# The near bias of the prompt's attention A added by VectorE instead of by identity matmuls

## The reference: what is computed

```python
logits = jnp.einsum('btkgd,btjkd->btkgj', qg, k_sel).astype(f32) * (D_A ** -0.5)
rel = s_pos[idx] - t_pos[None, :, None]
bias = bias_a[t5_bucket(rel)].astype(f32)
...
logits = jnp.where(valid[:, :, None, None, :], logits + bias, NEG)
p = jax.nn.softmax(logits, axis=-1).astype(v.dtype)
o = jnp.einsum('btkgj,btjkd->btkgd', p, v_sel)
```

## Time and profile before

| | |
|---|---|
| time before, median of 3 runs | 3327.85 us (3327.27 to 3331.41) |
| profiled execution: its time, its span | 3328.81 us, 3327.0 us |
| busy over the span | PE 94%, PEld 83%, DVE 41%, ACT 27%, POOL 25% |
| attention A of the prompt, units 0 to 63 | about 2203 to 2402 us of the span |
| last landmark before it | PE's matmuls of the projection end at 2188 us |

### The profile page before, as it was taken

One profiled execution on the slowest core, in us unless ns is written; L12 is line 12 of the kernel. 1 busy time (PEld: TensorE's weight loads), 2 busy tenths in 40 slices (PEclk: granted clock), 3 DMA queues, 4 the chain that ended last, 5 costly groups with the idle time before them and its releaser, 6 DMA issues. The chain is left out here.

```text
span 3327.0 us, 46645 instructions
## 1 busy us (share of the span) xinstructions
PE 3114.0 (94%) x17789; PEld 2770.6 (83%) x17789; DVE 1356.6 (41%) x2253; ACT 913.3 (27%) x1905; POOL 838.4 (25%) x613
## 2 busy tenths in 40 slices
PE   5969999999999999999999999979867999989997
PEld 5969998898989889998999999867656999878875
DVE  5002565484848169501444444047643121120322
ACT  4112212223131131112333343135433111131422
POOL 1222221221212212222222222124312222133453
PEclk7989999999999999999999999979978999999999
DMA  4453222322222313333333333132126333263453
GB/s 148 84 106 88 78 77 59 81 61 74 65 71 65 84 51 105 87 90 98 97 110 104 100 108 88 57 105 77 54 68 195 121 107 121 69 232 90 158 161 104
DMA packets 380821, 324.23 MB, mean 97 GB/s; under 512 B 39016, under 2 KB 339592, under 8 KB 377144
## 3 DMA queue, kind: packets, MB, share of 16 engines
q1 hardware_dynamic: 362888, 267.40, 28.7%
q10 hardware_dynamic: 17776, 54.65, 5.0%
HBM read 243.16 MB, written 78.88 MB: 97 GB/s over the span
## 5 line engine op out<-in xcount | busy, mean ns | idle before, releaser
L627 PE MATMUL banks<-h_hi,w_in_tile_hi 128*128 128x288 f32 (+4 forms) x2608 | 590.8, 332 | 32.2 <-POOL w_in_tile_lo L510 29.8
L510 POOL TENSOR_TENSOR w_in_tile_lo<-w_in_tile_raw,w_in_tile_hi 128x512 fp32r<-128x512 f32 x228 | 298.0, 1309 | 1174.2 <-ACT w_in_tile_hi L530 1174.2
L627 PE MATMUL banks<-h_lo,w_in_tile_hi 128*128 128x288 f32 (+4 forms) x2608 | 588.0, 331 | 0.0
L627 PE MATMUL banks<-h_hi,w_in_tile_lo 128*128 128x288 f32 (+4 forms) x2608 | 587.2, 331 | 0.0
L627 PEld LDWEIGHTS banks<-h_hi,w_in_tile_hi 128*128 128x128 f32 (+1 forms) x2608 | 442.3, 188 | 67.8 <-issue 34.1
L627 PEld LDWEIGHTS banks<-h_lo,w_in_tile_hi 128*128 128x128 f32 (+1 forms) x2608 | 446.9, 188 | 35.6 <-issue 0.4
L627 PEld LDWEIGHTS banks<-h_hi,w_in_tile_lo 128*128 128x128 f32 (+1 forms) x2608 | 446.7, 188 | 35.7 <-issue 0.4
L530 ACT CAST w_in_tile_hi<-w_in_tile_raw 128x512 fp32r<-128x512 f32 x228 | 141.6, 621 | 1008.6 <-PE banks L627 937.0
L792 DVE MAX8 top<-score 128x8 f32<-128x384 f32 (+6 forms) x224 | 247.1, 1103 | 33.0 <-DVE score L795 1.1
L1220 PE MATMUL banks<-h_hi,w_in_tile_hi 128*128 128x288 f32 (+1 forms) x1056 | 234.4, 330 | 9.7 <-PEq L133 5.5
L795 DVE MATCH_REPLACE8 score<-top,score 128x384 f32<-128x384 f32 (+6 forms) x224 | 243.0, 1085 | 0.0
(11 more groups left out here) (245 smaller groups left out, 4368.9 us busy)
## 6 DMA issues: line engine op xcount, KB each, us to landing
w_in_tile_raw<-in_w_in SPq DMA_DIRECT2D x312, 256.0 KB, 2.9
w_out_tile_raw<-in_w_out SPq DMA_DIRECT2D x128, 256.0 KB, 2.9
product<-spill ACTq DMA_DIRECT2D x48, 544.0 KB, 3.4
work<-product SPq DMA_DIRECT2D x32, 544.0 KB, 6.5
product<-g_spill ACTq DMA_DIRECT2D x22, 544.0 KB, 2.7
g_q_raw<-product SPq DMA_DIRECT2D x68, 128.0 KB, 2.8
merged<-work ACTq DMA_DIRECT2D x16, 544.0 KB, 7.7
x_rows<-in_x_prompt SPq DMA_DIRECT2D x8, 1024.0 KB, 5.2
```

The source lines that it names most:

```text
L510: pool.tensor_tensor(s.w_lo[:, q, :, :], s.w_raw[:, q, :, :], s.w_hi[:, q, :, :].bitcast(F32), ALU.subtract).then_inc(lo_made, 1)
L627: last = pe.matmul(ps[0:m, 3 * slot + c, 0:w], w_[:, q, kq, 0:m], h_[:, k, t0:t0 + w], start=(k == 0 and w_ is s.w_hi and h_ is s.h_hi), s ...
```

## The change

For the prompt alone, the two identity matmuls on the near table go, and with them the split of the table (two casts on ACT, two subtractions on DVE, the tiles near_hi and near_lo) and the waits of PE for it. DVE takes the logits with a new function `take_prompt`: the far columns of a chunk as before, the near columns with a scalar_tensor_tensor (logits + far + near), which keeps no maximum; the maximum over the near columns comes from a tensor_reduce over `prob`, and a second one, behind a new wait (`near_max`), joins it to the maxima of the far parts. The sample keeps its path.

```diff
             else:
                 k_lo_of(0)
                 q_lo_of(0)
-                for part, heads in enumerate(table_parts):
-                    near_lo_of(part, heads)
...
+            def take_prompt(n):
+                u = units[n][1]
+                if n in (0, PER):
+                    dve.wait_ge(table_in[n // PER], 16)
+                w_all = width[units[n][0]]
+                near_at = max(0, w_all - NEAR)
+                far_chunks = 0
+                for j, (c0, w) in enumerate(chunks(n)):
+                    c = first_chunk[n] + j
+                    n0 = min(max(c0, near_at), c0 + w)
+                    dve.wait_ge(logits_done, c + 1)
+                    if n0 > c0:
+                        far_chunks += 1
+                        last = dve.tensor_scalar(prob[:, n % RING, c0:n0], ps[:, c % 3, 0:n0 - c0], far[:, u:u + 1],
+                                                 None, ALU.add, ALU.max, accum_out=chunk_max[:, n % RING, j:j + 1])
+                    if n0 < c0 + w:
+                        t0 = n0 - (w_all - NEAR)
+                        last = dve.scalar_tensor_tensor(out=prob[:, n % RING, n0:c0 + w], in0=ps[:, c % 3, n0 - c0:w],
+                                                        scalar=far[:, u:u + 1], in1=near[:, u, t0:t0 + c0 + w - n0],
+                                                        op0=ALU.add, op1=ALU.add)
+                    last.then_inc(chunk_out, 1)
+                dve.wait_ge(chunk_out, first_chunk[n + 1])
+                dve.tensor_reduce(chunk_max[:, n % RING, far_chunks:far_chunks + 1], prob[:, n % RING, near_at:w_all], AX.X,
+                                  ALU.max).then_inc(near_max, 1)
+                dve.wait_ge(near_max, n + 1)
+                dve.tensor_reduce(neg_max[:, n % RING:n % RING + 1], chunk_max[:, n % RING, 0:far_chunks + 1], AX.X, ALU.max,
+                                  negate=True).then_inc(max_made, 1)
...
                     n0, n1 = max(c0, w_all - NEAR_W), c0 + w
-                    if n0 < n1:
+                    if sample and n0 < n1:
                         t0 = n0 - (w_all - NEAR_W)
                         for part in (near_hi, near_lo):
                             pe.matmul(bank[:, n0 - c0:w], s.ident_r[:, :], part[:, u, t0:t0 + n1 - n0], start=False,
```

More of the change, by code:

```diff
@@ L1350, in attend_a @@
         near = sb("near", [P, 2 * PER, NEAR_W])
-        near_hi = sb("near_hi", [P, 2 * PER, NEAR_W], F32R)
-        near_lo = sb("near_lo", [P, 2 * PER, NEAR_W], F32R)
+        if sample:
+            near_hi = sb("near_hi", [P, 2 * PER, NEAR_W], F32R)
+            near_lo = sb("near_lo", [P, 2 * PER, NEAR_W], F32R)
         far = sb("far", [P, 2 * PER])
@@ L1367, in attend_a @@
         (own_k_in, v_in, far_in, kT_done, k_hi_made, k_made, v_hi_made, v_made, near_hi_made, table_made, q_in0, q_in1, q_hi_made, q_made, mask_in0, mask_in1,
-         logits_done, chunk_out, max_made, exp_done, inv_made, scaled_pool, scaled_dve, turned, pt_hi_made, pt_made, pv_done, z_in0,
+         logits_done, chunk_out, near_max, max_made, exp_done, inv_made, scaled_pool, scaled_dve, turned, pt_hi_made, pt_made, pv_done, z_in0,
          z_in1, u_made, u_stored0, u_stored1, masks_set) = semaphores(nc, ctx, *[f"{x}_{tag}" for x in (
              "own_k_in", "v_in", "far_in", "kT_done", "k_hi_made", "k_made", "v_hi_made", "v_made", "near_hi_made", "table_made", "q_in0", "q_in1", "q_hi_made",
-             "q_made", "mask_in0", "mask_in1", "logits_done", "chunk_out", "max_made", "exp_done", "inv_made", "scaled_pool", "scaled_dve", "turned",
+             "q_made", "mask_in0", "mask_in1", "logits_done", "chunk_out", "near_max", "max_made", "exp_done", "inv_made", "scaled_pool", "scaled_dve", "turned",
              "pt_hi_made", "pt_made", "pv_done", "z_in0", "z_in1", "u_made", "u_stored0", "u_stored1", "masks_set")])
@@ L1557, in _ @@
                 q_hi_of(0)
-                for part, heads in enumerate(table_parts):
-                    act.wait_ge(table_in[part], 16)
-                    act.copy(near_hi[:, heads, :], near[:, heads, :]).then_inc(near_hi_made, 1)
                 act.wait_ge(k_in[1], 16)
@@ L1600, in take_logits, with take_sample @@
                     dve.wait_ge(turned, first_bank[n - RING + 1])
+                if sample:
+                    take_sample(n)
+                else:
+                    take_prompt(n)
+            def take_sample(n):
+                u = units[n][1]
                 for j, (c0, w) in enumerate(chunks(n)):
@@ L1696, in logits @@
                     pe.wait_ge(k_made, 1 if n == 0 else 2)
-                if not sample and n in (0, PER):
-                    pe.wait_ge(table_made, n // PER + 1)
                 if u == 0:
```

## The result

| | before | after |
|---|---|---|
| median of 5 runs each | 3327.85 us (3326.65 to 3331.41) | 3345.52 us (3344.74 to 3348.04) |
| ratio after to before | | 1.0052, 95% interval 1.0038 to 1.0067 |
| span of the profiled execution | 3327.0 us | 3343.6 us |
| first cast of k_hi_p to last u_out_p ("the stage") | 2196.7 to 2401.6, 204.9 us | 2195.6 to 2420.9, 225.3 us |
| what stands behind the stage | 925.4 us | 922.7 us |

The kernel is slower by 0.52%, 17.7 us. I measure the stage from the start of ACT's first cast of the keys to the start of DVE's last gate, since both landmarks are in every kernel here. It grew by 20.4 us. The span grew by less, 16.6 us, because the stage began 1.1 us sooner and because what follows it was 2.7 us shorter in this profile. The code behind the stage is the same in all kernels here.

A forecast was written before the change was run, and what follows sets the result against it. The prediction took DVE's sequence, not PE, to set the pace in attention A: +10.9 us in units 3 to 31 and +4.5 in blocks 4 to 7, together +15.4 on 3327.85, giving 3343 us, range 3331 to 3354.

The forecast's parts named there:

- DVE's loop: Prompt's attention A: take, maximum, exponential, reciprocal, next take closes over DVE and ACT without PE and sets the pace.
- Rival 1: Attention A: PE's relief decides and DVE's additions lie under its idle time; about 17 us faster, 3311 us; chance 0.08.
- The waits for exponentials: DVE's waits in attention A, 5.5 us then 3.7 us; forecast to hang on DVE's own maximum.
- Rival 2: Attention A: waits for exponentials absorb half, additions at lower bound; about +3 us, 3331, no change; chance 0.15.
- The additions: DVE time added per take: +0.26 us in block 0, up to +0.53 in blocks 2, 3, 6, 7; 28.9 us altogether.
- Units 3 to 31: Blocks 0 to 3: DVE's added time less its remaining 1.75 us of waits for PE, +10.9 us.
- The start: Stage start: first exponential stays where it is because ACT's cast waits for its transfer; gain nothing.
- Blocks 4 to 7: Seven steps from meet to meet, two takes on the chain, less PE's 0.24 us each: +4.5 us.
- the last group: End of the stage, with no logits behind it: forecast to add 0.
- The 0.6 us that PE was to have in hand: Blocks 4 to 7: about half a microsecond of PE's slack in perhaps two of seven steps, taken off the sum.
- rival 3: Mainly blocks 3 to 6: PE's gaps lower its clock, four to eight more slow stretches, +7 to +13 us; chance 0.12.
- What I said would show it: Stage ends about 15 us later, DVE's pt_hi waits shrink, PE's prob_p waits exceed 10 us, new instructions near 415 ns.

The follow-up runs named there:

- e2: Kernel before with DVE's new take alone, PE's near-table matmuls and the table's split kept: 3344.1 us, ratio 1.0063.
- e1: Kernel before without PE's identity matmuls on the near table, DVE's take unchanged: 3324.83 us, ratio 1.0002.
- e4: Kernel before with ACT casting the high part of the next block's queries one unit earlier: 3317.48 us, ratio 0.9978.
- e6: Changed kernel, far added into the near table at the start, tensor_tensor replacing the scalar_tensor_tensor, separate reduce kept: 3341.3 us, ratio 1.0051.
- e3: Changed kernel with the near tensor_reduce over one column instead of 128 or 256: 3333.22 us, ratio 1.0025.
- e5: Changed kernel, far added into the near table at the start, near addition and maximum in one tensor_tensor_reduce: 3325.38 us, ratio 1.0.
- e8: Changed kernel with one-pass near addition and maximum, queries' high part cast a unit earlier, reciprocal moved behind the take: 3303.35 us, ratio 0.9938.

## Why the prediction was right

The forecast was 3343 us, and the median is 3345.5: the mechanism held, and the sum of 15.4 us was too small for what the stage lost, 20.4. That the time came so near to the forecast is in part luck. The sum was one for the stage; the earlier start and the shorter rest (1.1 and 2.7 us), neither of them forecast, took back most of the 5.0 us that it lacked.

**DVE's loop sets the pace: shown.** e2, with DVE's half alone, loses what the change loses. e1, with PE's half alone, gains nothing measurable. e4 gains 0.22% from a wait of DVE for ACT. Rival 1 is thereby out. (Its DVE idle time of 22 to 32% should read 15 to 32%: in the third stretch of the earlier trace rows DVE is busy for 85%.) The Trainium skill (Perfetto Trace Analysis, Identifying the Most-Contended Engine) tells to optimize the engine with the highest occupancy first, but to judge TensorE by the share of its weight loads and by its FLOP use, not by matmul busy time. By matmul busy time PE led, with 86 to 96%. By its weight loads it has 78, 73, 78 and 79% against DVE's 68, 78, 85 and 76: level, with DVE ahead in two stretches. The runs show DVE to be the one that decides.

**The waits for exponentials take nothing up: shown.** They were 5.5 us in blocks 0 to 3 and are 6.0, and 3.7 us later and are 4.3. Rival 2 lived on them.

**The additions: right, with one price too low.** An iteration of block 6 on DVE after, to be laid beside the earlier trace rows:

```profile
2349.62 0.75 DVE L1628 TENSOR_SCALAR_CACHE_REDUCE prob_p<-banks,far_p 128x512 f32<-128x512 f32 x1
...
2350.30 0.35 DVE L1628 TENSOR_SCALAR_CACHE_REDUCE prob_p<-banks,far_p 128x128 f32<-128x128 f32 x1
...
2350.57 0.48 DVE L1632 SCALAR_TENSOR_TENSOR prob_p<-banks,far_p,near_p 128x256 f32<-128x256 f32 x1
2351.09 0.42 DVE L1637 TENSOR_REDUCE chunk_max_p<-prob_p 128x1 f32<-128x256 f32 x1
2351.54 0.16 DVE L1640 TENSOR_REDUCE neg_max_p<-chunk_max_p 128x1 f32<-128x3 f32 x1
2351.61 1.01 DVE L1656 TENSOR_TENSOR pt_lo_p<-banks,pt_hi_p 128x512 fp32r<-128x512 f32 x2
```

From the first take to the start of turned_lo are 1.99 us where it was 1.41: +0.58, forecast +0.53. The reduce starts 0.04 behind the end of the instruction that it waits for, and the next 0.03 behind its end, where the forecast had 0.05. The prices themselves, DVE's forms 2200 to 2410 us:

```profile
L1637 DVE TENSOR_REDUCE chunk_max_p<-prob_p 128x1 f32<-128x256 f32 x56 | 23.5, 420 | 1.9
L1632 DVE SCALAR_TENSOR_TENSOR prob_p<-banks,far_p,near_p 128x256 f32<-128x256 f32 x48 | 23.0, 479 | 0.0
...
L1632 DVE SCALAR_TENSOR_TENSOR prob_p<-banks,far_p,near_p 128x128 f32<-128x128 f32 x24 | 7.6, 343 | 2.8 <-DMA far_p<-in_rel_bias 2.8
...
L1637 DVE TENSOR_REDUCE chunk_max_p<-prob_p 128x1 f32<-128x128 f32 x8 | 2.3, 286 | 0.3
```

The reduce is 420 and 286 ns (forecast 415 and 280). The scalar_tensor_tensor is 479 and 343, not the 415 and 281 of the subtraction. I had named a take's price as the upper bound, and that is what it costs. e6 puts the error at 2.5 to 2.9 us of the stage.

**Units 3 to 31: +10.9 forecast.** PE's mask matmul that waits for the queries of block 4 began at 2268.06 before. After:

```profile
2278.20 0.60 PE L1737 MATMUL banks<-mask_p,ident_b 128*128 128x512 bf16 x1 [2.21 <-DVE q_lo_p L1580]
```

That is 10.1 us later, although the first exponential came 0.8 sooner: +11.0 from there. With the measured prices the same sum would be 4 x 0.31 + 8 x 0.46 + 16 x 0.60 - 1.75 = 12.8. So the sum is some 1.8 us too high but for the price that was too low, and its hit is in part luck; which of its terms was too high, no run shows.

**The start: right.** ACT's cast still waits for its transfer, and the first exponential comes 11.6 us after the stage's start, 11.3 before (0.3 us of what the stage lost):

```profile
2205.80 1.47 ACT L1560 CAST k_hi_p<-k_raw_p 128x1536 fp32r<-128x1536 f32 x1 [7.60 <-DMA k_raw_p<-product]
2207.18 0.40 ACT L1529 ACTIVATE prob_p<-prob_p,neg_max_p 128x128 f32<-128x128 f32 x1
```

**Blocks 4 to 7: the term that was mis-sized.** Forecast +4.5 over seven steps from meet to meet and 0 for the last group. From the seventh meet (start 2269.85 before, 2280.65 after) the seven steps grew by 1.43, 1.60, 0.66, 1.57, 1.17, 0.94 and 0.59 us, 8.0 together, and the two behind them by 0.45 and 0.02. Three things make the difference. The dearer instruction stands in two takes of each step, some 0.13 a step, 0.9 in all; in e6, without it, the seven steps grew by 1.4 us less. The 0.6 us that PE was to have in hand, and a last group at no cost, didn't come. And there are three stretches at half clock. One begins at the matmul shown above, which takes 0.60 us where it took 0.39 before. Another, in the step of 1.57 us; first PE's timeline at its start, then the windows around it (columns as above):

```profile
2334.33 0.28 PE L1737 MATMUL banks<-mask_p,ident_b 128*128 128x256 bf16 x1 [2.06 <-DVE prob_p L1628]
...
2336.24 0.60 PE L1737 MATMUL banks<-mask_p,ident_b 128*128 128x512 bf16 x1
```

```profile
2332.90:2336.30 3.40, 1.41 (x12) 1.17 (x12) 3.33 (x10) 1.07 (x4) 2.20 (x1) 0.99 0.00 0
2336.30:2339.70 3.40, 3.40 (x11) 2.60 (x10) 3.17 (x9) 1.85 (x5) 2.20 (x1) 0.50 0.55 147
2339.70:2343.00 3.30, 3.30 (x16) 2.70 (x15) 2.70 (x9) 0.00 (x0) 0.00 (x0) 1.00 0.58 169
```

PE waited 2.06 us for a take. Soon behind that the granted clock was 0.50, 1.2 GHz, for 3.4 us, and then 1.00 again. The third stretch begins at 2305.5, behind a wait of 2.19 us, in the step of 1.60. Before, there was none after 2268. This is rival 3's mechanism. From the matmul above to the seventh meet another 0.7 us is lost, and the steps of 1.60 and 1.57 stand some 0.7 and 0.9 over what the additions give or their neighbour shows, together about 2 us.

No run takes the low clock away by itself, but in e6 one stretch falls into another step. The same two steps, from the tenth and from the twelfth meet, first in after and then in e6:

```profile
2322.47:2339.23 16.76, 13.81 (x74) 10.77 (x72) 14.38 (x39) 8.75 (x18) 7.71 (x4) 0.91 0.22 61
2354.71:2372.46 17.75, 14.59 (x80) 11.36 (x79) 15.20 (x44) 9.02 (x17) 7.79 (x4) 1.00 0.16 48
```

```profile
2321.68:2337.39 15.71, 12.58 (x73) 9.73 (x72) 13.27 (x36) 8.17 (x17) 6.83 (x4) 1.00 0.18 53
2352.50:2370.93 18.43, 15.73 (x79) 12.21 (x79) 15.75 (x47) 9.58 (x18) 8.62 (x4) 0.91 0.20 56
```

The step with the clock at 0.91 is the longer one each time, by 0.9 and 0.8 us when 0.13 is allowed for e6's cheaper instruction. That agrees with the estimate. It doesn't part the low clock from the long wait of PE ahead of it, so the number stays argued. e2 and e3 have three such stretches too between 2270 and 2410 us, e1 and e5 one.

So the 5.0 us that the stage lost beyond the forecast are: 0.3 at the start, 0.1 in units 3 to 31, 4.1 in blocks 4 to 7 (about 1 for the price, 0.6 for PE's half microseconds that weren't in hand, some 2 argued, the clock; what is left is no more than these estimates are good for), and 0.5 in the last group.

**Rival 3 came true in its count, not in its price.** In blocks 0 to 3, from 2224 us on, the granted clock was 0.50 in two stretches of 3.4 us before and is so in two of 6.8 us after. With the three later ones that is five times 3.4 us more, within the "four to eight more" that the rival had in blocks 3 to 6 and that were to cost 7 to 13 us. The cost seen is about 2 us. In blocks 0 to 3 DVE waits for turned parts only 1.3 us alDVE waits for turned parts only 1.3 us in spite of the slow PE: PE is off the path there, and its slow clock doesn't show in the stage. there: what the slow clock costs an engine off the path doesn't show in the stage.

**What I said would show it.** DVE's waits for pt_hi: 1.3 us before block 5, and 7.8 in 6 waits later, so 1.3 each: right. PE's waits for a take "over 10 us": 9.5. The new instructions at 415 ns: the reduce yes, the other not. The stage 15 us later: 19.3. DVE's busy time up by 29 us: up by 25.6, with 2.5 us of subtractions on the table gone (the forecast of 28.9 counted the additions alone).

**What the gain was lost to.** The change pays for two cheap matmuls with a second pass over the columns, on the engine that sets the pace. The Trainium skill (VectorE: DVE Perf Modes, Rules for kernel authors) calls tensor_reduce the slowest DVE instruction and advises to restructure where it is on a hot path; the trace has it at 420 ns for 256 columns, level with a tensor_tensor of that size that reads PSUM (419), though a tensor_scalar from SBUF to SBUF is quicker (347, the additions to the table in e5 and e6). It is the second pass that costs. The advice holds: e5, which restructures it, takes 21.6 us off the 225.3 of the stage.

## What to carry to other kernels

Ask of a busy engine whether it waits for the others or they for it. Here PE was busy for 93% of the stretch and 9 us less of it gave no time that can be measured; DVE, at 77%, gave 7 us for one kind of wait taken away. When work moves to the engine whose sequence sets the pace, count passes over the columns: an addition and its maximum in one pass made the same move neutral, and with DVE's waits taken off it became a gain. Price an unseen instruction by the dearest kin in the trace, and look at what the other engine's longer gaps do to its clock.

## What the runs showed of the hardware

- A scalar_tensor_tensor that takes fp32 from PSUM with a table in SBUF costs 479 ns for 256 columns and 343 for 128. The tensor_tensor on the same operands costs 419 and 282. The difference is 60 ns at both lengths, and the take (tensor_scalar with a maximum) stands as high, 478 and 345. What the 60 ns are for is not shown. It isn't a second arithmetic step as such, since the addition with a maximum below has one and costs 419; the scalar_tensor_tensor and the take both read a scalar for each partition (`far`), and the two cheaper ones don't.
- The addition with a running maximum (tensor_tensor_reduce, add and max) costs 419 and 283 ns, no more than the plain addition. Its accumulator is read in 82 ns, and in e8 the reduce that waits for it starts 0.47 us after its start.
- A tensor_reduce over columns in SBUF costs 420 ns for 256, 286 for 128 and 154 for one.
- In blocks 4 to 7 of after, the granted clock was 0.50 for about 3.4 us behind PE's waits of 2.21, 2.19 and 2.06 us for DVE (the last ending at 2334.33), up to 2 us after their end. Behind a fourth wait of 2.06 us (ending at 2367.84, below) it stayed at 1.00. So the length of the wait alone doesn't decide it.

```profile
2367.84 0.34 PE L1737 MATMUL banks<-mask_p,ident_b 128*128 128x384 bf16 x1 [2.06 <-DVE prob_p L1628]
```
